# Launch order, chunk pairs behind the norms, the last residual tile and the output of a two-block kernel

## The reference

```python
def rms_norm(x, w, eps=RMS_EPS):
    y = xf * lax.rsqrt(jnp.mean(xf * xf, axis=-1, keepdims=True) + eps)
    return (y * w).astype(x.dtype)

def hybrid_layer(x, ...):                 # first block, two layers
    h = rms_norm(x, norm_w)
    proj = h @ w_in                       # 14352 columns: attention, conformer, delta rule, gates
    ...                                   # three branches
    merged = g_a * y_a + g_c * y_c + g_d * y_d
    return x + merged @ w_out

# second block, two layers; layer 0 also carries a context of 256 tokens beside x
h = modulate(rms_norm_2(x, norm_mix[layer]), shift1, scale1)
q, k, v, hy, g = jnp.split(h @ w_in[layer], PROJ_SPLITS, axis=-1)
x = x + gate1 * merge_branches(attn, hyo, g, ...)
x = x + gate2 * swiglu(modulate(rms_norm_2(x, norm_ffn[layer]), shift2, scale2), w_gate_up, w_down)
# at the end
return rms_norm_2(x, norm_final)
```

## Time and profile before

| | |
|---|---|
| median of three runs | 2594.8 us |
| the profiled execution | 2594.07 us |
| span of its trace | 2592.3 us |
| mean granted clock of TensorE, 1.0 is 2.4 GHz | 0.993 |
| busy share: PE, PEld, DVE, ACT, POOL | 97%, 83%, 44%, 48%, 55% |

### The profile page before, as it was taken

How to read it: one execution, slowest core, us unless ns; L and a number is a source line. 1 busy time by engine, 2 the same in 40 slices (tenths; PEclk the granted TensorE clock), 3 DMA queues, 4 the chain that set the end, 5 groups by cost and what they waited for, 6 DMA issues and landing times.

```text
span 2592.3 us, 42001 instructions
## 1 busy us (share of the span) xinstructions
PE 2505.7 (97%) x16564; PEld 2161.5 (83%) x16564; DVE 1128.1 (44%) x2170; ACT 1237.1 (48%) x2104; POOL 1437.2 (55%) x827
## 2 busy tenths in 40 slices
PE   6999999999999999999899999999999999999997
PEld 6998889888999889988577766768888868898997
DVE  7895645444977654536325512331101123535013
ACT  5457654355446764436544411443323345645543
POOL 5875746456976655446432222646565545564960
PEclk9999999999999999999999999999999999999999
DMA  5544343445544343345321112232222223245553
GB/s 224 191 163 147 131 163 132 146 168 185 185 164 162 131 173 132 135 151 207 135 80 51 49 65 84 86 112 84 95 98 98 94 101 130 83 146 178 182 183 143
DMA packets 50552, 347.63 MB, mean 134 GB/s; under 512 B 5312, under 2 KB 8640, under 8 KB 8896
## 3 DMA queue, kind: packets, MB, share of 16 engines
q1 hardware_dynamic: 47840, 340.31, 36.7%
q10 hardware_dynamic: 2528, 4.72, 0.6%
HBM read 343.96 MB, written 1.05 MB: 133 GB/s over the span
## 4 chain that ended last, share of the span: by engine, by line
PE 88%; DVE 5%; ACT 3%; DMA 1%; issue 1%; POOL 1%; SPq 0%; ACTq 0%; DVEq 0%; POOLq 0%
PE pg L1909 23%; PE pg L1911 22%; PE pg L1910 22%; PE pg L1934 2%; PE ps L2212 2%; PE ps L2233 2%; PE pg L1932 2%; PE ps L2231 1%; PE ps L2370 1%; PE ps L2351 1%; ACT ring_hi L767 1%; DMA ring<-in_w_stream_dram 1%; PE ps L2061 1%; PE ps L2067 1%; DVE H L1335 1%
## 5 line engine op out<-in xcount | busy, mean ns | idle before, releaser
L654 POOL TENSOR_TENSOR ring_lo<-ring,ring_hi 128x1024 fp32r<-128x1024 f32 (+4 forms) x496 | 1153.4, 2339 | 747.9 <-ACT ring_hi L767 746.0
L1909 PE MATMUL pg<-HH,ring_hi 128*128 128x256 f32 (+1 forms) x3360 | 1079.1, 321 | 39.1 <-DVE HL L1306 14.3
L1910 PE MATMUL pg<-HH,ring_lo 128*128 128x256 f32 (+1 forms) x3360 | 1025.9, 305 | 0.0
L1911 PE MATMUL pg<-HL,ring_hi 128*128 128x256 f32 (+1 forms) x3104 | 953.6, 307 | 0.0
L1909 PEld LDWEIGHTS pg<-HH,ring_hi 128*128 128x128 f32 x3360 | 637.6, 190 | 121.9 <-issue 56.0
L1910 PEld LDWEIGHTS pg<-HH,ring_lo 128*128 128x128 f32 x3360 | 638.6, 190 | 45.4 <-issue 17.7
L1911 PEld LDWEIGHTS pg<-HL,ring_hi 128*128 128x128 f32 x3104 | 589.6, 190 | 30.7
L767 ACT ACTIVATE ring_hi<-ring 128x1024 fp32r<-128x1024 f32 (+6 forms) x564 | 555.4, 1002 | 41.9 <-DMA ring<-in_w_stream_dram 37.4
L777 ACT ACTIVATE take<-pg 128x256 f32<-128x256 f32 (+1 forms) x244 | 104.5, 428 | 481.1 <-PE pg L1911 429.6
L1911 PE MATMUL pg<-big_r,ring_hi 128*128 128x256 f32 (+1 forms) x864 | 274.0, 317 | 0.0
L1909 PE MATMUL pg<-big_r,ring_hi 128*128 128x256 f32 (+1 forms) x736 | 239.8, 326 | 4.8 <-DVE ring_lo L1634 2.7
(11 more groups left out here) (328 smaller groups left out, 3180.0 us busy)
## 6 DMA issues: line engine op xcount, KB each, us to landing
ring<-in_w_stream_dram SPq DMA_DIRECT2D x320, 1024.0 KB, 4.8
hn<-in_consts_dram ACTq DMA_DIRECT2D x2, 1024.0 KB, 5.3
cst<-in_consts_dram SPq DMA_DIRECT2D x1, 1472.0 KB, 19.6
prm<-in_params_dram SPq DMA_DIRECT2D x1, 1110.0 KB, 7.4
X<-in_xT_dram SPq DMA_DIRECT2D x1, 1024.0 KB, 5.7
X<-in_ctxT_dram ACTq DMA_DIRECT2D x1, 1024.0 KB, 7.2
out_dram<-H ACTq DMA_DIRECT2D x1, 1024.0 KB, 4.8
cst<-in_consts_dram SPq DMA_DIRECT2D x1, 768.0 KB, 16.5
```

What stands on the lines that cost most here:

```text
L654: pool.tensor_tensor(ring_lo[:, slot, cols], ring[:, slot, cols], ring_hi[:, place * P:(place + n) * P].bitcast(F32), SUB).then_inc(sem(LO ...
L1909: first = pe.matmul(out, a[0], b[0], start=start, stop=False)
L1910: pe.matmul(out, a[1], b[0], start=False, stop=False)
L1911: return first, pe.matmul(out, a[0], b[1], start=False, stop=stop)
```

## The change

It has nine parts, all of them in the order or the place of work; no arithmetic is dropped.

1. SyncE brings ring slot 0 ahead of the parameters and the positions.
2. At launch ScalarE loads the root's table right behind the squares, splits only the two pieces of chunks `ag` 0 and 1, takes the root, and splits the pieces of slot 1 behind the fourth rounding of H. VectorE makes the low parts of the first two pieces.
3. At norm 3 ScalarE splits only the pieces of `k2` 0 and 1 ahead of the root; the third (of `q2` 0) comes later.
4. The function `pair` interleaves the two chunks behind each norm tile by tile: tile c of both before tile c+1 of either.
5. The last of the eight residual tiles (`LAST_ADDS`) doesn't pass through `take` and GpSimd: VectorE adds it from PSUM to X.
6. VectorE adds seven squares only; the eighth goes into the sum as a second matmul with ones (L2107 of the changed kernel).
7. The Exp of lambda and the Silu of the condition move on ScalarE from behind chunk 3 to behind chunk 7 of `ag`, and VectorE's use of lambda moves behind the second pair of convolutions.
8. In `updates`, ScalarE calls `ahead` for the last chunk in place of draining it.
9. The output goes in four DMAs of two tiles each.

```diff
+LAST_ADDS = [(name, l, KD * FF_PARTS[l] - 1 if name == "down" else KD - 1)
+             for name, l in (("w_out", 0), ("w_out", 1), ("w_out2", 0), ("down", 0), ("w_out2", 1), ("down", 1))]
...
-    if name == "w_out" and i < 2:
+    if name == "w_out" and i < 2 or name == "ag" and l == 0 and i < 2:
...
+            sp.dma_start(ring[:, 0, :], w_stream[0]).then_inc(sem("weights0"), 16)
             sp.dma_start(prm[:, :], params).then_inc(sem("loaded"), 16)
             sp.dma_start(ANGI, pos).then_inc(sem("loaded"), 16)
-            for s in range(RING):
+            for s in range(1, RING):
...
+                    if (name, l, first + m) in LAST_ADDS:
+                        continue
...
+                elif i and m == KD - 1:
+                    act.wait_ge(sem("x_last"), (1, 2, 4, 5, 6, 7).index(i) + 1)
...
-                    ahead(CHUNK[NORM_USER[i]] - 1)
-                if i != 3:
+                    ahead(CHUNK[NORM_USER[i]] - 1, CHUNK[NORM_USER[i]] + (1 if i == 3 else len(ORDER)))
+                if i not in (0, 3):
...
-                    if m < KD:
+                    if m < KD - 1:
                         put(m)
+                    elif m == KD - 1:
+                        ahead(CHUNK[LAST_OF[i]])
...
-            ahead(0)
+            log_exp_tables()
+            ahead(0, CHUNK["ag", 0, 1])
             norm_root(0)
             for k in range(KD):
+                if k == KD // 2:
+                    ahead(0)
                 high_part(0, k)
...
-            act.wait_ge(sem("norm_h"), 8 * KD)
-            act.dma_start(out, H[:, :, 0:T]).then_inc(sem("stored"), 16)
-            act.wait_ge(sem("stored"), 16)
+            for k in range(0, KD, 2):
+                act.wait_ge(sem("norm_h"), 7 * KD + k + 2)
+                act.dma_start(out[:, k:k + 2, :], H[:, k:k + 2, 0:T]).then_inc(sem("stored"), 16)
+            act.wait_ge(sem("stored"), 64)
...
+                    ahead(CHUNK["ag", 0, 0])
...
-                for k in range(2, KD):
+                for k in range(2, KD - 1):
                     if i == ffn_norm[1]:
                         ahead(CHUNK["w_out2", DEPTH - 1, min(k + 2, KD - 1)])
                     link(ins)
                     dve.wait_ge(sem("norm_sq"), KD * i + k + 1)
-                    ins = dve.tensor_tensor(ps[:, 1, 0:n] if k < KD - 1 else rstd[:, 0:n], ps[:, 1, 0:n], H[:, k, 0:n], ADD)
+                    ins = dve.tensor_tensor(ps[:, 1, 0:n] if k < KD - 2 else rstd[:, 0:n], ps[:, 1, 0:n], H[:, k, 0:n], ADD)
                 ins.then_inc(sem("norm_sum"), 1)
+                if i in LAST_OF:
+                    name, l, j = LAST_OF[i]
+                    bank = pg[:, CHUNK[name, l, j] % 4, :]
+                    dve.wait_ge(sem("chunk_ready"), CHUNK[name, l, j] + 1)
+                    for t in (slice(a, a + T) for a in range(0, N_TOK[l] if name != "w_out" else T, T)):
+                        if name == "w_out":
+                            ins = dve.tensor_tensor(X[:, KD - 1, t], bank[:, t], X[:, KD - 1, t], ADD)
+                        else:
+                            gate = (2 if name == "w_out2" else 5) * KD + KD - 1
+                            ins = dve.scalar_tensor_tensor(X[:, KD - 1, t], bank[:, t], mod[:, l, gate, t.start // T:t.start // T + 1],
+                                                           X[:, KD - 1, t], MUL, ADD)
+                    ins.then_inc(sem("x_last"), 1)
...
+            def pair(name, l, k, rhs, n, arrived):
+
+                j = CHUNK[name, l, 0]
+                assert j == at["chunk"] and CHUNK[name, l, 1] == j + 1
+                at["chunk"] += 2
+                freed, w = at["free"], []
+                for c in range(k):
+                    arrived(c)
+                    for q in range(2):
+                        if c == 0:
+                            bank_free(j + q)
+                            w.append([tile(split=True) for _ in range(k)])
+                        first, ins = parts(pg[:, (j + q) % 4, 0:n], w[q][c], rhs(c), c == 0, c == k - 1)
+                        if c == q == 0 and freed:
+                            first.then_inc(sem("slot_free"), freed)
+                            at["free"] -= freed
+                        if c == k - 1:
+                            ins.then_inc(sem("chunk_ready"), 1)
...
-                pe.matmul(ps[:, 0, 0:n], ones, rstd[:, 0:n], start=True, stop=True).then_inc(sem("norm_ss"), 1)
+                pe.matmul(ps[:, 0, 0:n], ones, rstd[:, 0:n], start=True, stop=False)
+                pe.wait_ge(sem("norm_sq"), KD * (i + 1))
+                pe.matmul(ps[:, 0, 0:n], ones, H[:, KD - 1, 0:n], start=False, stop=True).then_inc(sem("norm_ss"), 1)
...
+                pair("gu", l, KD, hx, n, normed(ffn_norm[l]))
```

More of the change, by code:

```diff
@@ L755, in _, with ahead @@
             split = [0]
-            def ahead(j):
-                while split[0] < len(PIECES) and PIECES[split[0]][4] <= HELD.get(j, j):
+            def ahead(j, until=len(ORDER)):
+                while split[0] < len(PIECES) and PIECES[split[0]][4] <= HELD.get(j, j) and PIECES[split[0]][8] <= until:
                     t, n, place, reader, step, who, count = PIECES[split[0]][:7]
@@ L1587, in delta, with ahead @@
                 ins.then_inc(sem("d_vb"), 1)
+            split = [0]
+            def ahead(j):
+                while split[0] < len(PIECES) and PIECES[split[0]][4] <= HELD.get(j, j):
+                    t, n, place, reader, step, who, count = PIECES[split[0]][:7]
+                    split[0] += 1
+                    if not who:
+                        continue
+                    cols = slice(t % TILES * P, (t % TILES + n) * P)
+                    slot = t // TILES % RING
+                    dve.wait_ge(sem("high_ready"), split[0])
+                    dve.tensor_tensor(ring_lo[:, slot, cols], ring[:, slot, cols],
+                                      ring_hi[:, place * P:(place + n) * P].bitcast(F32), SUB).then_inc(sem(LOW_READY[1]), 1)
             dve.wait_ge(sem("x_loaded"), 16)
@@ L1620, in rope @@
                 dve.tensor_tensor(qk, cut(at_buf, 0, 2, T), turned, ADD).then_inc(sem("rope"), 1)
-            split = [0]
-            def ahead(j):
-                while split[0] < len(PIECES) and PIECES[split[0]][4] <= HELD.get(j, j):
-                    t, n, place, reader, step, who, count = PIECES[split[0]][:7]
-                    split[0] += 1
-                    if not who:
-                        continue
-                    cols = slice(t % TILES * P, (t % TILES + n) * P)
-                    slot = t // TILES % RING
-                    dve.wait_ge(sem("high_ready"), split[0])
-                    dve.tensor_tensor(ring_lo[:, slot, cols], ring[:, slot, cols],
-                                      ring_hi[:, place * P:(place + n) * P].bitcast(F32), SUB).then_inc(sem(LOW_READY[1]), 1)
             def modulation(l, part):
@@ L2274, in _ @@
                 hx = parts_of(HH, HL, T)
-                for i in range(16):
-                    chunk("ag", l, i, KD, hx, T, normed(l) if i == 0 else None)
-                    if l and i == 1:
-                        fill(norm_mods(l, "turns"))
+                pair("ag", l, KD, hx, T, normed(l))
+                if l:
+                    fill(norm_mods(l, "turns"))
+                for i in range(2, 16):
+                    chunk("ag", l, i, KD, hx, T)
                 for i in range(16):
@@ L2377, in _ @@
                 i = HN_BASE2[l]
-                for j in range(2):
-                    chunk("k2", l, j, KD, parts_of(HH, HL, 2 * T), 2 * T, normed(mix_norm[l]) if j == 0 else None)
+                pair("k2", l, KD, parts_of(HH, HL, 2 * T), 2 * T, normed(mix_norm[l]))
                 fill(norm_mods(mix_norm[l], "turns"))
@@ L2465, in _ @@
                 per = KF // FF_PARTS[l]
+                pair("gu", l, KD, hx, n, normed(ffn_norm[l]))
                 for i in range(KF):
[L2467 to L2468 removed]
+                    for half in range(2 if i else 0):
+                        chunk("gu", l, 2 * i + half, KD, hx, n)
                     if i == 0:
```

30 lines of the change are left out of this document (17 added, 13 removed).

## The result

| | before | after |
|---|---|---|
| median of four runs | 2594.6 us | 2564.9 us |
| ratio, 95% interval | | 0.988 (0.9867 to 0.9892) |
| profiled execution | 2594.07 us | 2564.82 us |
| span of its trace | 2592.3 us | 2562.9 us |

The change gains 29.7 us, 1.1%; forecast were 2564.1 us and 30.7 us. The medians say nothing of the places, so I compare the starts of one instruction that stands behind each norm in both traces, the turn of the modulation's row (L1950 before, L2003 after). What the lead grows by from one of these to the next is what the stretch gave.

The account below looks back on a forecast made before the run. TensorE, busy 97% of the span, was taken as the bound. Gains 6.6 + 1.6 + 8.3 + 4.5 + 4.4 + 2.3 + 3.4 = 31.1 us, less 0.4, gave 2563.4 profiled, median 2564.1 us; range 2555 to 2574.

Parts of the forecast that it names:

- Launch: At launch: slot 0 lands earlier, H starts at 13.85, TensorE at 15.55, pair ends at 25.0; gain 6.6 us (4.5 to 8.4).
- so I keep the fall: norm 1 1.6: At norm 1: TensorE still idles 4.4 us before the pair, so its clock still falls; gain 1.6 us, not 3.2.
- Norms 2 and 3: At norm 3: root follows the sum instead of a DMA wait, pair ends at 1280.0 against 1288.30; gain 8.3 us.
- the step on the missing idle stretch: At norm 3: TensorE goes from filling straight to the pair, so its clock doesn't fall; gain 4.9 us if it does.
- Norms 4 and 5: At norms 4 and 5: the pair's work fills nearly all waits for tiles, start unchanged; gains 4.5 and 4.4 us.
- the sign to look for: At norms 4 and 5: the modulation's row turns 11 to 11.5 us behind the pair's first matmul.
- Norm 6: At norm 6: pair starts at 2382.3, ends at 2388.1 at full clock, 2391.4 with the whole fall; gain 2.3 us (1.0 to 4.8).
- End: Last norm and store: H starts 1.0 us earlier, the store in pieces saves 2.4; gain 3.4 us (2.4 to 4.2).
- The rest: In the chunks of `ag`: a TensorE that comes earlier may catch up with GpSimd's low parts; 0.4 us taken off.
- GpSimd as the bound in `ag`: Rival: in dense runs of `ag`, `gu`, TensorE waits for GpSimd and its clock falls; about 2615 us, chance 0.02.
- Pairs that wait as before: Rival: at the pairs each tile's HL still ends last, 4.5 + 4.4 + 3.9 fall away; gain 18, 2576 us, chance 0.05.
- The clock that falls nowhere: Rival: TensorE's clock falls behind no norm, 31.1 + 1.6 + 2.5 + 1.1 = 36.3; time 2558 us, chance 0.14.

Follow-up runs that it names:

- e5_store: The changed kernel with the output leaving in one DMA again once all eight tiles are there; 2568.1 us.
- e2_launch: The changed kernel with the old launch order (parameters before weights, all four splits before the root, low parts on GpSimd), interleaved pair kept; 2567.7 us from three executions.
- e7_fill: The changed kernel plus eight idle matmuls behind the sum at norms 1 and 6, in TensorE's pause; 2559.2 us.
- e4_last: The changed kernel with the last residual tile through ScalarE and GpSimd again, all eight squares added by VectorE, one matmul for the sum; 2568.1 us.
- f1_delta: The changed kernel plus fifteen short idle matmuls in TensorE's pauses at the delta gates of both layers; 2565.1 us.
- e6_first: The changed kernel with two pieces of weights rounded before the last residual tile's square at norms 1 and 4 to 6, `HELD` lifted; 2560.4 us.

## Why the prediction was right, and where it was off

The mechanisms held: an earlier root at the launch and at norm 3, pairs that fill TensorE's waits for tiles, a store that overlaps VectorE. That the median came within 1 us is in part luck: norm 1, norms 2 and 3 and the rest fell short by 2.4 us together, the other places gave 1.1 us more, and the four executions alone spread over 3.3 us.

- **Launch**, forecast 6.6, gave 6.9. The steps landed within 0.3 us (H, TensorE's start); HL 5 was late behind GpSimd's low parts as forecast, and the pair ended at 24.9 (forecast 25.0). Undone alone, the pieces are worth 3.8 (order) and 2.0 (pair); some 1 us comes only from both together.
- **Norm 1**, forecast 1.6, gave 0.6. The step "so I keep the fall: norm 1 1.6" was mis-sized: it kept one of 3.4 us, and the fall was 6.8 us long. Where the fall was 3.4 us (`e5_store`), sum to marker took 13.3 us instead of 14.5, which makes the gain 1.7. The last square came 0.86 us earlier than the lead before it, forecast 0.75.
- **Norms 2 and 3**, forecast 8.3, gave 7.6, 8.3 of it behind norm 3's sum. Both edits are needed: behind norm 3's sum the pair with the old bound gave 1.5 us, the bound without the pair 4.7. The clock stayed up there, as the step on the missing idle stretch had it. The rest, -0.7, is norm 2, with the wait near 1173 us, which of the other runs only `e5_store` has. Without that wait, and with the second matmul, nine experiments take 0.1 to 0.8 us less there than the kernel before.
- **Norms 4 and 5**, forecast 4.5 and 4.4, gave 4.6 and 4.7, but not as split. The pair is worth 3.7, not 4.5; the last tile's shorter way, put at nothing against its second matmul, is worth 1.0 net. Two errors cancelled. By the rows, the pair at norm 4 started 0.8 us earlier than before, counted from norm 3's marker, and took 12.0 us where the sum has 11.2 and the sign to look for 11 to 11.5: VectorE brings a tile each 1.57 us, and TensorE's 1.4 us of work per tile don't hide all of that.
- **Norm 6**, forecast 2.3, gave 2.4, with the whole fall of 6.8 us. The number is right by luck: with the whole fall the forecast's own working leaves 1.5 (2391.4 against 2392.88), and 2.3 is a value between that and the 4.8 without a fall for which it shows no working. With 3.4 us of it the stretch gave 3.5 (`e2_launch`), with none 4.4 (`e7_fill`).
- **End**, forecast 3.4, gave 3.7: 2.6 by the stores (2.4 forecast), 1.1 by the rest (1.0). Undone in `e4_last`, parts 5 and 6 cost 1.7 us there and not 1.1; why is open.
- **The rest** lost 1.1 us against 0.4 forecast, and not by the step that had it, a TensorE that catches up with GpSimd. It lies in the two layers' attention (0.3 and 0.8 us), where the falls at the delta gates were 6.8 us long instead of 3.4; with these falls gone, `f1_delta` had 0.4 and 0.9 us back.
- **Rivals.** GpSimd as the bound in `ag` did not come: TensorE's six waits for its low parts sum to 6.2 us, before 5.7 in seven. Pairs that wait as before did not come either: undoing them costs 14.9 us. The clock that falls nowhere, put at 36.3 us, is now seen: `e7_fill` takes the falls at both norms away and gains 4.6 us there, where the rival had 1.6 + 2.5. It takes an edit to get there; in the changed kernel they came.
- Part 8 does nothing, as forecast; `e6_first` shows about what it would give if `HELD` let it through.

What stays open: why a fall lasts 3.4 us in one run and 6.8 in another behind the same pause, and what brings the one near 563 us, which nine of the fourteen traces have and five don't, and those near 1175 us, which two have. Each is seen in one profiled execution, so a length or a fall says nothing of a kernel's other executions.

## What to carry to other kernels

Compare two traces by markers behind each stage, since the gains of a change of many parts are read there and its errors cancel in the sum. Price a dense stretch behind a pause at half clock, not at full, and test filling the pause with matmuls whose result nobody uses: it cost nothing and gave 2 to 2.6 us at each norm. But first see whether TensorE bounds that stretch, since where others pace it, as at the delta gates, the clock is worth little, and where it lets TensorE run ahead into new pauses, as at launch, it can lose.
